# Stage-end norms of a two-block transformer kernel: squares in two tiles, sums between output blocks, lead panels block by block

## What is computed

```python
def _layer_norm(x, g, b):
    xf = x.astype(F32)
    mu = jnp.mean(xf, axis=-1, keepdims=True)
    var = jnp.mean(jnp.square(xf - mu), axis=-1, keepdims=True)
    y = (xf - mu) * lax.rsqrt(var + LN_EPS)
    return (y * g.astype(F32) + b.astype(F32)).astype(x.dtype)

def _sq_relu_mlp(h, w1, w2):
    return jnp.square(jax.nn.relu(h @ w1)) @ w2

def _swiglu(x, w_gate, w_up, w_down):
    return (jax.nn.silu(x @ w_gate) * (x @ w_up)) @ w_down

h = _layer_norm(DEEPNORM_ALPHA * h + mix, ln_g[layer, 0], ln_b[layer, 0])
h = _layer_norm(DEEPNORM_ALPHA * h + _sq_relu_mlp(h, ffn_w1[layer], ffn_w2[layer]), ln_g[layer, 1], ln_b[layer, 1])
```

## Time and profile before

| | us |
|---|---|
| median of three runs | 2914.92 |
| lowest and highest | 2911.51, 2915.75 |
| the profiled execution | 2912.68 |
| its span | 2910.9 |

### The profile page before, as it was taken

How to read it: one execution, slowest core, us unless ns; L and a number is a source line. 1 busy time by engine, 2 the same in 40 slices (tenths; PEclk the granted TensorE clock), 3 DMA queues, 4 the chain that set the end, 5 groups by cost and what they waited for, 6 DMA issues and landing times.

```text
span 2910.9 us, 39840 instructions
## 1 busy us (share of the span) xinstructions
PE 2758.6 (95%) x16514; PEld 2401.7 (83%) x16514; DVE 1287.9 (44%) x2144; ACT 1030.4 (35%) x1624; POOL 300.8 (10%) x357
## 2 busy tenths in 40 slices
PE   8899999999999999999999999997987899999997
PEld 6787899999988888888888888877876787888886
DVE  4444553333432332654334433345666644533333
ACT  4544343222322232443223422224556543422221
POOL 0000200000200000300002100013112221200003
PEclk9999999999999999999999999998998999999998
DMA  3111233222122212232221322222211212232220
GB/s 133 44 52 38 80 110 108 90 88 80 37 66 66 92 54 80 80 123 94 94 94 59 129 94 94 94 74 71 95 58 45 94 37 79 81 108 94 95 65 30
DMA packets 66532, 232.96 MB, mean 80 GB/s; under 512 B 8880, under 2 KB 9264, under 8 KB 65968
## 3 DMA queue, kind: packets, MB, share of 16 engines
q1 hardware_dynamic: 66352, 230.41, 24.2%
HBM read 228.25 MB, written 2.10 MB: 79 GB/s over the span
## 4 chain that ended last, share of the span: by engine, by line
PE 83%; DVE 6%; ACT 5%; POOL 3%; issue 2%; DMA 0%; SPq 0%; DVEq 0%; POOLq 0%; ACTq 0%
PE ps L542 72%; POOL R L2487 2%; PE ps L847 2%; PE ps L562 1%; PE ps L552 1%; PE ps L724 1%; PE ps L685 1%; POOL S L2476 1%; DVE HT L1800 1%; PE ps L834 1%; PE ps L575 1%; DVE XL L1790 1%; ACT HT L1168 1%; PE ps L1041 1%; DVE SCR L2308 1%
## 5 line engine op out<-in xcount | busy, mean ns | idle before, releaser
L542 PE MATMUL ps<-XH,WH 128*128 128x264 f32 (+2 forms) x1856 | 544.8, 336 | 13.1 <-DVE XL L2450 8.9
L542 PE MATMUL ps<-XH,LENT 128*128 128x512 f32 (+2 forms) x2096 | 524.5, 343 | 6.2 <-DVE XL L1790 6.2
L542 PE MATMUL ps<-XL,WH 128*128 128x264 f32 (+2 forms) x1856 | 528.5, 327 | 0.0
L542 PE MATMUL ps<-XH,WL 128*128 128x264 f32 (+2 forms) x1856 | 527.2, 326 | 0.0
L542 PE MATMUL ps<-HH,LENT 128*128 128x264 f32 (+2 forms) x2220 | 499.4, 322 | 7.4 <-DVE HL L1760 7.4
L1753 DVE TENSOR_TENSOR WL<-RAW,WH 128x1024 fp32r<-128x1024 f32 (+1 forms) x232 | 285.6, 1231 | 273.7 <-ACT WH L1138 273.2
L542 PEld LDWEIGHTS ps<-XH,LENT 128*128 128x128 f32 x2096 | 356.9, 191 | 56.1 <-DVE XL L1790 8.9
L542 PEld LDWEIGHTS ps<-HH,LENT 128*128 128x128 f32 x2220 | 368.5, 194 | 37.4 <-issue 7.6
L542 PEld LDWEIGHTS ps<-XH,WH 128*128 128x128 f32 x1856 | 323.9, 192 | 54.0 <-issue 17.4
L542 PEld LDWEIGHTS ps<-XH,WL 128*128 128x128 f32 x1856 | 323.0, 192 | 28.5
L542 PEld LDWEIGHTS ps<-XL,WH 128*128 128x128 f32 x1856 | 323.3, 192 | 26.5
(11 more groups left out here) (226 smaller groups left out, 2773.1 us busy)
## 6 DMA issues: line engine op xcount, KB each, us to landing
RAW<-in_wf SPq DMA_DIRECT2D x128, 512.0 KB, 3.3
RAW<-in_wr SPq DMA_DIRECT2D x48, 512.0 KB, 3.3
RAW<-in_wg SPq DMA_DIRECT2D x44, 512.0 KB, 3.3
RAW<-in_wu SPq DMA_DIRECT2D x44, 512.0 KB, 3.3
RAW<-in_wd SPq DMA_DIRECT2D x32, 512.0 KB, 3.2
RAW<-in_we SPq DMA_DIRECT2D x24, 512.0 KB, 3.3
RAW<-in_wm SPq DMA_DIRECT2D x24, 512.0 KB, 3.3
RAW<-in_wro SPq DMA_DIRECT2D x16, 512.0 KB, 3.4
```

Of the source, the lines that this page charges most:

```text
L542: mm = e.matmul(o[:, at:at + m], wt, xt[:, k, c0 + a * m:c0 + (a + 1) * m], start=(n == 0 and j == 0), stop=(n == nk - 1 and j == 2))
```

## The change

- VectorE adds squares 6 and 7 too (`add_square`), behind the eighth centre. The stat pass reads two tiles in place of four.
- TensorE does 17 steps between total and stat pass where it did 11, and 6 before the total of half 0 (11 before) and 8 of half 1 (9 before). ScalarE and VectorE do 6 and 8 before theirs, 5 in place of 3 behind root and reciprocal, and 3 in place of 1 after each block of the output loop.
- GpSimd does the end sums of half 0 first. Those of half 1 come in the norm of half 0: two behind the square adds, one behind r_out 0, 3 and 6 (ln00 has one less).
- The second lead pass runs on TensorE over all lead panels k-block by k-block. Each panel keeps its own bank of PSUM meanwhile.
- ScalarE and VectorE plan ahead once more, `ah.ahead(ah.panel)`, before they evict the second lead pass.

The diff, without its empty lines in other places and the same edit of `down_norm` in VectorE's program:

```diff
@@ -586,11 +586,8 @@
             o = bank(("total", ln, half), 1, (S.mean, ln, half))
             w.wait_ge(*mark)
             e.matmul(o[:, 0:T], ONE[:, :], sums, start=True, stop=True).then_inc(*S.total(ln, half))
-            pump(8)
-            pump(3)
-            ht = [HT[:, i, 0:T] for i in (1, 2, 3, 4)]
-            rstd((ln, half), [(ht[0], S.add_pool[(ln, half, 4)]), (ht[1], S.add_dve[(ln, half, 6)]),
-                              (ht[2], S.sq[(ln, half, 6)]), (ht[3], S.sq[(ln, half, 7)])],
+            pump(17)
+            rstd((ln, half), [(HT[:, 1, 0:T], S.add_pool[(ln, half, 4)]), (HT[:, 2, 0:T], S.add_dve[(ln, half, 7)])],
                  T, (S.normed, ln, half, 7), pump, 3)
             pump(9)
             give(("bcast", (ln, half)))
@@ -615,7 +613,11 @@
                     freed = (S.q_copy, "crs", i, half)
                 else:
                     freed = (S.silu if name[1] == "g" else S.up, i, half)
-                yield from gemm(name, idx, X, x_ready(ln, half), c0 + half * T // 2, T // 2, freed, half)
+                yield gemm(name, idx, X, x_ready(ln, half), c0 + half * T // 2, T // 2, freed, half)
+
+        def in_turn(panels):
+            for g in panels:
+                yield from g
 
         def down_norm(ln, done=0, midway=None, other=None, order=range(8)):
 
@@ -641,12 +643,17 @@
             for half in (0, 1):
                 if half == 1:
                     drain(fill)
-                    fill = other() if other else lead_pass(ln, 0)
+                    fill = other() if other else in_turn(lead_pass(ln, 0))
                 c = c0 + half * T // 2
                 layer_norm(ln, half, T // 2, S1[:, c:c + T // 2], S.sum[sums_at(name, base + 7, half)], pumping(fill),
-                           9 if half else 11)
+                           8 if half else 6)
             drain(fill)
-            drain(lead_pass(ln, 1))
+            leads = list(lead_pass(ln, 1))
+            for k in range(8):
+                for g in leads:
+                    next(g)
+            for g in leads:
+                drain(g)
 
 
         def even_panel(t, kind, sig):
@@ -1164,19 +1171,19 @@
                 if k == 6:
                     w.wait_ge(*S.add_pool[ln, half, 2])
                 if k == 7:
-                    w.wait_ge(*S.add_dve[ln, half, 4])
+                    w.wait_ge(*S.add_dve[ln, half, 3])
                 e.activation(HT[:, SQ_SLOT[k], 0:T], res(k), ACT.Square).then_inc(*S.sq(ln, half, k))
                 pump(1)
             pump(3)
             root((ln, half), T, inv, LN_EPS)
-            pump(3)
+            pump(5)
             for k in range(9):
                 if k < 8 and dst:
                     w.wait_ge(*S.normed[ln, half, k])
                     w.wait_ge(*S.panel[final(AT[X_LAST[ln]])])
                     e.activation(XH[:, k, c:c + T], HT[:, T_SLOT[k], 0:T], ACT.Identity, bias=pcol(ln + "b", k),
                                  scale=pcol(ln + "g", k)).then_inc(*S.x_hi(ln, half, k))
-                pump(1)
+                pump(3)
             normed[0] = (ln, half, 7)
 
         def relu2(name, idx, c0, T, half):
@@ -1265,9 +1272,10 @@
                     drain(fill)
                     fill = other() if other else lead_pass(ln, 0)
                 c = c0 + half * T // 2
-                layer_norm(ln, half, T // 2, c, lambda k, c=c: R[:, k, c:c + T // 2], pumping(fill), 9 if half else 11, dst)
+                layer_norm(ln, half, T // 2, c, lambda k, c=c: R[:, k, c:c + T // 2], pumping(fill), 8 if half else 6, dst)
             drain(fill)
             ah.quiet = False
+            ah.ahead(ah.panel)
             drain(lead_pass(ln, 1))
 
         def down(name, base):
@@ -1767,21 +1775,26 @@
             e.reciprocal(st[0:wd, 6:6 + n], st[0:wd, 0:n]).then_inc(*S.recip(*key))
 
         def layer_norm(ln, half, T, c, res, ready, pump, first, dst):
+            def add_square(k):
+
+                w.wait_ge(*S.sq[ln, half, k])
+                if k > 3:
+                    w.wait_ge(*S.add_dve[ln, half, {5: 3, 6: 5, 7: 6}[k]])
+                e.tensor_tensor(HT[:, 2, 0:T], HT[:, 2, 0:T], HT[:, SQ_SLOT[k], 0:T],
+                                ALU.add).then_inc(*S.add_dve(ln, half, k))
             pump(first)
             for k in range(8):
                 w.wait_ge(*S.mean[ln, half])
                 w.wait_ge(*ready(k))
                 e.tensor_tensor(res(k), res(k), HT[:, 0, 0:T], ALU.subtract).then_inc(*S.centre(ln, half, k))
                 if k in (4, 6):
-                    a = SQ_SLOT[k - 1]
-                    w.wait_ge(*S.sq[ln, half, k - 1])
-                    if k == 6:
-                        w.wait_ge(*S.add_dve[ln, half, 4])
-                    e.tensor_tensor(HT[:, 2, 0:T], HT[:, 2, 0:T], HT[:, a, 0:T], ALU.add).then_inc(*S.add_dve(ln, half, k))
+                    add_square(k - 1)
                 pump(1)
+            add_square(6)
+            add_square(7)
             pump(3)
             recip((ln, half), T)
-            pump(3)
+            pump(5)
             spread = acc(("bcast", (ln, half)), 1)[:, 0:T]
 
             def lower(k):
@@ -2475,17 +2489,22 @@
                 w.wait_ge(*S.sum[sums_at(name, idx - 1, half)])
                 e.tensor_tensor(dst, dst, src, ALU.add).then_inc(*S.sum(i, half))
 
-        def layer_norm(ln, half, T, res, dst):
+        def layer_norm(ln, half, T, res, dst, between={}):
+
             for k, a in ((2, 3), (4, 5)):
                 w.wait_ge(*S.sq[ln, half, k])
                 if k == 4:
                     w.wait_ge(*S.add_pool[ln, half, 2])
                 e.tensor_tensor(HT[:, 1, 0:T], HT[:, 1, 0:T], HT[:, a, 0:T], ALU.add).then_inc(*S.add_pool(ln, half, k))
+            for m in between.get(-1, ()):
+                sums(*m)
             w.wait_ge(*S.par_in["par"])
             for k in range(8):
                 w.wait_ge(*S.normed[ln, half, k])
                 e.tensor_scalar(res(k), HT[:, T_SLOT[k], 0:T], pcol(ln + "g", k), pcol(ln + "b", k), ALU.mult,
                                 ALU.add).then_inc(*S.r_out(ln, half, k))
+                for m in between.get(k, ()):
+                    sums(*m)
 
         def down_norm(ln, dst=True):
             name, base, alpha, stage = end_of(ln)
@@ -2493,11 +2512,15 @@
             n_end = len(ENDS[ln])
             for m in range(8 - n_end):
                 sums(name, base + m, m, c0, T, None)
+            def ends(half):
+                return [(name, base + m, m, c0 + half * T // 2, T // 2, half) for m in range(8 - n_end, 8)]
+            for m in ends(0):
+                sums(*m)
+            second = ends(1)
+            between = {-1: second[0:2], 0: second[2:3], 3: second[3:4], 6: second[4:5]}
             for half in (0, 1):
                 c = c0 + half * T // 2
-                for m in range(8 - n_end, 8):
-                    sums(name, base + m, m, c, T // 2, half)
-                layer_norm(ln, half, T // 2, lambda k: R[:, k, c:c + T // 2], dst)
+                layer_norm(ln, half, T // 2, lambda k: R[:, k, c:c + T // 2], dst, {} if half else between)
 
         e.memset(ONE[:, :], 1.0).then_inc(*S.const("one"))
         e.memset(EP[:, 0:1], LN_EPS)
```

More of the change, by code:

```diff
@@ L1895, in down_norm @@
                 layer_norm(ln, half, T // 2, c, lambda k, c=c: R[:, k, c:c + T // 2],
-                           lambda k, half=half: S.res[sums_at(name, base + k, half)], pumping(fill), 9 if half else 11, dst)
+                           lambda k, half=half: S.res[sums_at(name, base + k, half)], pumping(fill), 8 if half else 6, dst)
             drain(fill)
             ah.quiet = False
+            ah.ahead(ah.panel)
             drain(lead_pass(ln, 1))
```

## The result

| | us |
|---|---|
| changed kernel, median of four runs | 2887.23 (2883.23 to 2888.87) |
| before, median of four runs | 2913.9 (2911.51 to 2915.75) |
| ratio | 0.9907, 95% interval 0.989 to 0.9924 |

A forecast was written before the change was run, and what follows sets the result against it. TensorE, busy 95% of the span, was taken as the bound, with its stands in the stage-end norms. The terms sum to a gain of 16.8 us, 2912.7 to 2896 us, with a range of 2873 to 2912.

The forecast's parts named there:

- C: Rival, chance 0.10: waits at every block put half the second lead pass at half rate, 2929 us; all of it, 67 lost.
- D: Rival, chance 0.20 together with B: the second half's total is not early because another step ends last; 2908 us.
- B: Rival, chance 0.20 together with D: queued lead evictions and splits delay the next stage's first panels in six norms; 2912 us.
- part 2: TensorE in the norms: 17 panel steps between total and stat pass, not 11, cover the stat pass's waits; +5.5 us.
- Part 1: Stat pass of the norms: two tiles of squares drop 152 records, less 1.5 us for unhidden VectorE adds; +12.2 us.
- Part 3: GpSimd's moved sums: 12.1 us of waits for totals go, 16.3 us of new stand for XL comes; -4.2 us.
- Part 4: Second lead pass block by block with three pumped steps: 10.3 us of waits go, 15.0 us of stand comes; -4.7 us.
- Parts 5 to 7: Earlier mean in ln4, +2.9 us; shorter waits in ln1 and the memory's norm, +1.0; later slots behind leads, -2.9.
- Part 8: TensorE's clock in six norms and ln4: lost stands spare the matmuls behind them the lower rate; +7 us.

The follow-up runs named there:

- e2: The kernel before with the two tiles of squares alone (VectorE adds squares 6 and 7); 2935.78 us against 2912.83, ratio 1.0073.
- e1: The changed kernel with four tiles of squares again, VectorE not adding squares 6 and 7; 2879.6 us, ratio 0.9892 to the kernel before.
- e7: The changed kernel with TensorE's step counts as before, the other engines' as changed; 2913.09 us, ratio 0.9991 to the kernel before.
- e3: The changed kernel with GpSimd's second-half sums again in one block behind the first half's r_outs; 2895.9 us, ratio 0.9943 to the kernel before.
- e4: The changed kernel with TensorE's second lead pass panel after panel, the three pumped steps kept; 2931.84 us, ratio 1.0061 to the kernel before.
- e5: The kernel before with only TensorE's second lead pass put in block order; 2900.98 us against 2917.24, ratio 0.9936.
- e9: The kernel before with throwaway matmuls on TensorE before its wait for the second half's total; 2913.29 us against 2913.3, ratio 0.9997.

## Why the prediction was right, and where its steps were not

The time lay in the range and on the side that was forecast, and rivals C and D did not happen (of B one wait, 1.67 us in ln01). The sum is 10 us short, and its terms are mostly wrong, two of them in sign. They made up for one another, and that the total came so near is luck. Right are the direction, the late total that the sums' new places bring forward, the steps of part 2, and the small terms.

**Part 1, two tiles (+12.2).** 152 records went, as said, and TensorE's work with them: 17.4 us, 0.115 a record, where I took 0.09. The step that failed is "one of them behind the last square [...] hidden by them": I priced the two adds at 0.5 us in three passes, and looked at square 7 as what they follow. In the second halves they follow the lead panel's eviction on VectorE. Measured: a loss of 18 us alone, and by stretches of about 7 in the changed kernel, which the ratios don't set apart from none (e2, e1). That TensorE has six steps more there to cover the adds is shown by e7; that the eviction moved ahead, behind centre 0, may help too, and no run shows it by itself.

**Part 2, 17 steps (+5.5).** Right in mechanism, mis-sized: 27 us when undone (e7). I counted only the waits that the kernel before shows. The adds of part 1 made the waits longer that these steps must cover; the rest of the difference I can't divide further.

**Part 3, sums (-4.2).** Sign wrong. Of the 12.1 us of total waits 10.0 went. The new stand, 16.3, did not come: in ln01 I had 2.4 and the trace has 1.35 of waits (742.82, 744.28 and 745.26), below the 2 to 4 that I had named as the sign of part 3. Over the whole kernel the XL wait is the same with and without the interleaving (e3). Undone it costs 9, with four tiles 19.5.

**Part 4, lead pass and pumping (-4.7).** Here I took 10.3 off and put 15.0 on. The whole kernel shows 11.9 for the first pass and the second together, where parts 3 and 4 have 31. The worth of the block order was the difference to a heavy loop in panel order, which I never worked out: 41.5 us (e4), and 10.8 with the light loop (e5). I costed the two edits against the waits of before, one at a time, and 28.5 us come only where both are made. Why they do I can only argue: steps that are pumped in the output loop are out of the chain in front of the stat pass, and the block order gives TensorE 1.46 us of work for each turn of the loop.

**Parts 5 to 7.** ln4: 2.9 and its share of part 1 forecast, 2.7 by stretches in all. ln1 with the memory's norm: 1.0 and a share of part 1, 3.2 in all. The slot of ln01: 2.0 forecast, 1.67 in the row at 770.83. These small ones, each worked out for one place, came out within 1.5 us.

**Part 8, clock (+7).** 10.1 us on the panel matmuls. Right in sign and a third short. It is the reverse of C: ln01 has no lower clock at all (1.00 in its window). My reason for it, that each stand costs the matmuls behind it, is not borne out as it stands: with the stands at the totals filled the time did not change (e9).

## What to carry to other kernels

When an edit makes an engine do one more thing for a chain, look at what is queued ahead of it on that engine, and not only at the event that it waits for: adds that I had priced at 0.5 us raised a wait from 0.5 to 2.6 us here, because an eviction stood in between. Parts that fill one another's gaps can't be costed each against the trace of before; work out at least the pair (here block order and heavier loop: -10.8 and +4.2 alone, -35.1 together). And a forecast whose total is right may rest on terms that are not; taking each part out once, one by one, pointed to a part that only cost, and with a later eviction to a kernel that is 13 us faster than the change by stretches.

## What the runs showed of the hardware

TensorE's clock behind a stand: with the stand at ln01's total filled by matmuls whose result is thrown away, the granted clock kept its 2.4 GHz there and fell to 1.2 GHz behind the next stat pass instead (rows of e9). The share of time at the lower clock fell (missing clock in the eight windows 46 us against 57), and the kernel's time didn't (0.9997).

Executions of one kernel differ in the clock that they are granted, and those with less of it are mostly longer: of 19 executions of the kernel before on one chip the shortest, 2909.3 us, has 0.977 and the longest, 2922.3 us, 0.972.
